# The residual's product on VectorE, four PSUM banks for the down-projection, and the second pair's weight-sum remainders on GpSimd, in a two-layer hybrid encoder step

## What is computed

```python
x = layer_norm(ALPHA * x + (1.0 + gate) * mix, ln_g, ln_b)
hin = x * (1.0 + scale) + shift
u = hin @ ffn_w_in + ffn_b_in              # 1024 -> 2 x 2816
u, hist = causal_dwconv(u, ffn_conv, ffn_conv_w)   # 3 taps
u = u + ffn_conv_b
f = (silu(u[..., :2816]) * u[..., 2816:]) @ ffn_w_down
x = layer_norm(ALPHA * x + (1.0 + gate) * f, ln_g2, ln_b2)
```

## Time and profile before

| | us |
|---|---|
| median of 3 runs (lowest to highest) | 3170.7 (3169.97 to 3174.64) |
| the profiled execution | 3175.71 |
| its span | 3173.9 |
| TensorE busy | 2951.9 (93%) |
| VectorE busy | 2312.7 (73%) |
| ScalarE busy | 1227.5 (39%) |
| GpSimd busy | 986.5 (31%) |
| one pass of the FFN loop (2806.54 to 2875.18) | 68.64 |

### The profile page before, as it was taken

How to read it: one execution, slowest core, us unless ns; L and a number is a source line. 1 busy time by engine, 2 the same in 40 slices (tenths; PEclk the granted TensorE clock), 3 DMA queues, 4 the chain that set the end, 5 groups by cost and what they waited for, 6 DMA issues and landing times. The chain is left out here.

```text
span 3173.9 us, 51760 instructions
## 1 busy us (share of the span) xinstructions
PE 2951.9 (93%) x18516; PEld 2792.6 (88%) x18516; DVE 2312.7 (73%) x3500; ACT 1227.5 (39%) x2360; POOL 986.5 (31%) x653
## 2 busy tenths in 40 slices
PE   7999989999998999999998879989998999999995
PEld 5999977999988999999997868878988999999994
DVE  7999966777459777788877556645277788887775
ACT  3333244554345332333333634444155333333224
POOL 2333435665315222223222121110323222222222
PEclk9999989999999999999999999999999999999998
DMA  6545653110111111111111210002201111111111
GB/s 265 176 171 180 227 193 109 54 54 21 54 34 34 47 53 40 45 48 46 46 46 35 90 42 34 35 28 79 78 21 47 41 47 46 48 44 52 41 40 56
DMA packets 86969, 225.75 MB, mean 71 GB/s; under 512 B 9388, under 2 KB 41076, under 8 KB 85812
## 3 DMA queue, kind: packets, MB, share of 16 engines
q1 hardware_dynamic: 46900, 139.10, 12.9%
q10 hardware_dynamic: 39936, 84.86, 7.8%
HBM read 192.59 MB, written 31.35 MB: 71 GB/s over the span
## 5 line engine op out<-in xcount | busy, mean ns | idle before, releaser
L370 POOL TENSOR_TENSOR WL<-RAW,WH 128x1024 fp32r<-128x1024 f32 x193 | 511.5, 2651 | 975.2 <-ACT WH L365 975.1
L374 PE MATMUL PS<-HH,WH 128*128 128x352 f32 x2120 | 704.1, 332 | 61.7 <-POOL WL L370 22.6
L378 PE MATMUL PS<-HH,WL 128*128 128x352 f32 x2120 | 689.8, 325 | 0.0
L377 PE MATMUL PS<-HL,WH 128*128 128x352 f32 x2120 | 689.3, 325 | 0.0
L374 PEld LDWEIGHTS PS<-HH,WH 128*128 128x128 f32 x2120 | 405.4, 191 | 79.4 <-issue 62.4
L2113 DVE SCALAR_TENSOR_TENSOR X<-PS,ADA,X 128x352 f32<-128x352 f32 (+1 forms) x704 | 326.7, 488 | 167.8 <-PE PS L378 162.5
L377 PEld LDWEIGHTS PS<-HL,WH 128*128 128x128 f32 x2120 | 406.4, 192 | 1.8
L378 PEld LDWEIGHTS PS<-HH,WL 128*128 128x128 f32 x2120 | 405.6, 191 | 0.0
L365 ACT ACTIVATE WH<-RAW 128x1024 fp32r<-128x1024 f32 x199 | 210.2, 1056 | 385.7 <-PE PS L374 378.8
L374 PE MATMUL PS<-FH,WH 128*128 128x352 f32 x960 | 325.2, 339 | 28.2 <-DVE X L2113 28.0
L378 PE MATMUL PS<-FH,WL 128*128 128x352 f32 x960 | 310.4, 323 | 0.0
(11 more groups left out here) (384 smaller groups left out, 6281.7 us busy)
## 6 DMA issues: line engine op xcount, KB each, us to landing
RAW<-ws SPq DMA_DIRECT2D x199, 512.0 KB, 3.3
ADR<-wada ACTq DMA_DIRECT2D x72, 512.0 KB, 4.8
scr<-V ACTq DMA_DIRECT2D x32, 528.0 KB, 3.0
X<-xT SPq DMA_DIRECT2D x3, 1408.0 KB, 20.7
OUTT<-scr SPq DMA_DIRECT2D x1, 4224.0 KB, 15.3
y<-X SPq DMA_DIRECT2D x3, 1408.0 KB, 5.5
AD0R<-wada SPq DMA_DIRECT2D x8, 512.0 KB, 13.3
AD<-wada SPq DMA_DIRECT2D x2, 2048.0 KB, 15.1
```

The costliest lines, as they stand in the source:

```text
L370: e.tensor_tensor(WL[u][:, :], RAW[:, u, :], WH[u][:, :].bitcast(fp32), ALU.subtract).then_inc(lo_done, 1)
L374: mm = e.matmul(out, WH[w][:, c:c + 128], mh, start=first, stop=False)
L377: e.matmul(out, WH[w][:, c:c + 128], ml, start=False, stop=False)
L378: return e.matmul(out, WL[w][:, c:c + 128], mh, start=False, stop=last)
```

## The change

Five edits. (1) `pool_normal` on GpSimd becomes `vec_normal` on VectorE, three instructions behind the first `t_lower`s and ahead of convolution (0,1); it waits for the reciprocal (`std_rdy`) instead of `hl_rdy`. (2) The down-projection of all pairs but the last uses the four banks 6, 7, 1, 5, and group k waits for update k-4; at k == 2 TensorE also waits until the next pair's second block has left banks 1 and 5. To make room, `up_first` writes groups into banks 0 to 5 in its own order, the mixed block (1,1) uses banks 1, 2, 3, 4, 0, and later blocks wait, before they reuse bank 1 or 5, for all 24 updates. (3) The remainders `S1L` to `S4L` of each second block (j,1) are made by GpSimd: three behind slab n+2, the fourth behind slab n+3; the first two wait also until the sum that reads the one they overwrite is made. (4) The sums and the remainders of the next first block stand behind updates 9, 11, ... 23 of `mix`. (5) In `first_half`, L2141 stands ahead of the gate, and the four sums follow the gate together.

```diff
@@ -622,11 +622,11 @@
                 for m in range(KB - 2 if q % 2 == 0 else 1, KB - 1):
                     pool_sum(p, q, m, ch)
 
-        def pool_normal(p, q, ch):
+        def vec_normal(v, q, ch):
 
             c0, cw = CHS[ch]
-            p.wait_ge(hl_rdy, low_count(HS[q], 2))
-            p.tensor_tensor(X[:, :, c0:c0 + cw], X[:, :, c0:c0 + cw], LN_R[q][ch][:, 0:cw].unsqueeze(1).to_broadcast([128, KB, cw]),
+            v.wait_ge(std_rdy, 6 * q + 2 * ch + 2)
+            v.tensor_tensor(X[:, :, c0:c0 + cw], X[:, :, c0:c0 + cw], LN_R[q][ch][:, 0:cw].unsqueeze(1).to_broadcast([128, KB, cw]),
                             ALU.mult).then_inc(nrl_rdy, 1)
 
         def vec_center(v, q, ch, b):
@@ -1681,6 +1681,7 @@
             if not isinstance(count, int) or count > 0:
                 need(e, s_, count)
 
+        DN_BANKS = (6, 7, 1, 5)
         FIRST_ORDER = [(0, 1), (1, 1), (0, 0), (0, 2), (1, 0), (1, 2)]
 
         def pe_ffn(e, l, n0, g0, hs):
@@ -1695,15 +1696,15 @@
             def up_first(n):
 
                 b = 3 * (g0 + up_index(1, 0, 0))
-                for half, ch in FIRST_ORDER:
+                for i, (half, ch) in enumerate(FIRST_ORDER):
                     if (half, ch) in ((0, 1), (1, 1)):
                         need(e, hi_done, n + half + 1)
                         need(e, lo_done, n + half + 1)
                     c0, cw = CHS[ch]
                     u = (n0 + half) % 2
-                    need(e, up_ev, b - 6 + 3 * half + ch + 1)
+                    need(e, up_ev, b - 6 + i + 1)
                     for k in range(KB):
-                        mm = three(e, PS[:, 3 * half + ch, 0:cw], u, k * 128, HH[:, k, c0:c0 + cw], HL[:, k, c0:c0 + cw],
+                        mm = three(e, PS[:, i, 0:cw], u, k * 128, HH[:, k, c0:c0 + cw], HL[:, k, c0:c0 + cw],
                                    k == 0, k == KB - 1, k == 0 and (half, ch) in ((0, 1), (1, 0)))
                     mm.then_inc(up_done, 1)
 
@@ -1734,7 +1735,7 @@
                 q, b = mixed_pair(l, j, f), 3 * (g0 + up_index(j, f, 0))
                 head = isinstance(j, int) and (j, f) == (1, 1)
                 ua, ub = n0 % 2, (n0 + 1) % 2
-                A, C, B, E0, E1 = (5, 2, 3, 4, 0) if f and not head else (0, 1, 2, 3, 4)
+                A, C, B, E0, E1 = (1, 2, 3, 4, 0) if head else (5, 2, 3, 4, 0) if f else (0, 1, 2, 3, 4)
                 T_ = [(XTH[i], XTL[i], 0, 0) for i in range(3)] + [(HH, HL, 0, CW)]
                 S_ = [(SH[i], SL[i], 0) for i in range(4)]
                 B11, B21, B22 = (HH, HL, 0, 0), (HH, HL, 4, 0), (HH, HL, 4, CW)
@@ -1751,10 +1752,14 @@
                 if not f:
                     need(e, up_ev, b)
                     need(e, st_dv, 3 * q)
-                free(3)
+                elif not head:
+                    need(e, dn_ev, d0 + 3 * KB * (j - 1))
+                free(2)
                 product(A, A11, B11, True, up_done, True)
 
-                free(1, (st_dv, 3 * q - 2))
+                free(3, (st_dv, 3 * q - 2))
+                if not f:
+                    need(e, dn_ev, d0 + 3 * KB * (j - 1))
                 need(e, sl_rdy, sl_count(l, q, 1))
                 if head:
                     need(e, sl_rdy, tl_count(l, 0))
@@ -1778,7 +1783,7 @@
 
                 need(e, hi_done, n + 2)
                 need(e, lo_done, n + 2)
-                free(2, (up_ev, b))
+                free(1, (up_ev, b))
                 whole(E1, ub)
 
                 need(e, up_ev, b + 4)
@@ -1802,9 +1807,11 @@
                     u = (n0 + m // 4) % 2
                     for ch, (c0, cw) in enumerate(CHS):
                         k = 3 * m + ch
-                        need(e, dn_ev, d0 + 3 * KB * j + k - 1)
+                        after(e, dn_ev, d0 + 3 * KB * j + k - 3)
+                        if k == 2:
+                            need(e, up_ev, 3 * (g0 + up_index(j + 1, 1, 0)) + 6)
                         for f in range(2):
-                            mm = three(e, PS[:, 6 + k % 2, 0:cw], u, f * 512 + (m % 4) * 128, FH[:, f, c0:c0 + cw],
+                            mm = three(e, PS[:, DN_BANKS[k % 4], 0:cw], u, f * 512 + (m % 4) * 128, FH[:, f, c0:c0 + cw],
                                        FLS[f][:, c0:c0 + cw], f == 0, f == 1, m % 4 == 0 and ch == 0 and f == 0)
                         mm.then_inc(dn_ps, 1)
 
...
@@ -1953,7 +1960,7 @@
                     for k in range(4):
                         sum_upper(1, 1, k)
                     upper(0, 1)
-                copy_out(1, 0, half, (ch,), b1 + i + 1)
+                copy_out(1, 0, half, (ch,), b1 + i + 1, i)
 
             def second_half(j, n, first=()):
                 split(n, 3)
@@ -2036,22 +2043,30 @@
             p.memset(UF[:, :, 0:GAP], 0.0)
             p.memset(UF[:, :, GAP + SEQ:GAP + UT - DEC - (FC - 1)], 0.0)
             params(0, 0)
-            pool_normal(p, 2 * l, 0)
             split(n0, 2)
             tails(0, 0)
-            pool_normal(p, 2 * l, 1)
             split(n0, 3)
-            pool_normal(p, 2 * l, 2)
             params(0, 1)
             split(n0, 4)
             tails(0, 1)
             split(n0, 5)
+            def sum_lower(j, f, i):
+
+                q = mixed_pair(l, j, f)
+                need(p, tap_sh_rdy, sh_count(l, q, i + 1))
+                if i < 2:
+                    need(p, ss_rdy, ss_count(l, q, 2 * i + 2))
+                p.tensor_tensor(SL[i][:, :], SF[i][:, :], SH[i][:, :].bitcast(fp32), ALU.subtract).then_inc(sl_rdy, 1)
+
             def pair(j):
                 n = n0 + 4 + 6 * (j - 1)
                 params(j, 0)
                 split(n, 2)
+                for i in range(3):
+                    sum_lower(j, 1, i)
                 tails(j, 0)
                 split(n, 3)
+                sum_lower(j, 1, 3)
                 params(j, 1)
                 split(n, 4)
                 tails(j, 1)
@@ -2105,21 +2120,21 @@
                 need(v, ft_rdy, x + 1)
                 v.tensor_tensor(FLS[f][:, :], FT[:, f, :], FH[:, f, :].bitcast(fp32), ALU.subtract).then_inc(fl_rdy, 1)
 
-            def update(j, k, m, ch):
+            def update(j, k, m, ch, banks=DN_BANKS):
 
                 c0, cw = CHS[ch]
                 need(v, dn_ps, d0 + 3 * KB * j + k + 1)
                 for a, w, st in pieces(c0, cw):
-                    ins = v.scalar_tensor_tensor(X[:, m, a:a + w], PS[:, 6 + k % 2, a - c0:a - c0 + w],
+                    ins = v.scalar_tensor_tensor(X[:, m, a:a + w], PS[:, banks[k % len(banks)], a - c0:a - c0 + w],
                                                  ADA[:, s, 2 * KB + m, st:st + 1], X[:, m, a:a + w], ALU.mult, ALU.add)
                 ins.then_inc(dn_ev, 1)
 
-            def mix(j, steps=iter(()), first=0):
+            def mix(j, steps=iter(()), places=range(1, 3 * KB, 3)):
 
                 need(v, x_rdy, 6 * l + 3)
                 for k in range(3 * KB):
                     update(j, k, k // 3, k % 3)
-                    if k % 3 == 1 and k >= first:
+                    if k in places:
                         next(steps, None)
                 for _ in steps:
                     pass
...
@@ -2178,6 +2193,13 @@
                 need(v, tap_sh_rdy, sh_count(l, mixed_pair(l, j, f), i + 1))
                 v.tensor_tensor(SL[i][:, :], SF[i][:, :], SH[i][:, :].bitcast(fp32), ALU.subtract).then_inc(sl_rdy, 1)
 
+            def w_splits(j):
+
+                yield from w_sums(j, 0)
+                for i in range(4):
+                    sum_lower(j, 0, i)
+                    yield
+
             def t_sums():
 
                 lq, mode = 2 * l, MODE[HS[2 * l]]
@@ -2254,21 +2276,19 @@
             gate(0, 0)
             for i in (0, 2, 1):
                 t_lower(i)
+            for ch in range(NCH):
+                vec_normal(v, 2 * l, ch)
             every_step(conv(0, 1))
             t_lower(3)
             v.wait_ge(nrl_rdy, 3 * l + 3)
             every_step(w_sums(1, 1))
             lower(0, 0)
             gate(0, 1)
-            for i in range(4):
-                sum_lower(1, 1, i)
             lower(0, 1)
 
             def second_half(j):
                 every_step(conv(j, 0))
                 mixed_out(j, 1, 0)
-                if not isinstance(j, int) or j > 1:
-                    sum_lower(j, 1, 3)
                 gate(j, 0)
                 mixed_out(j, 1, 1)
                 mixed_out(j, 1, 2)
@@ -2277,31 +2297,22 @@
                 every_step(conv(j - 1, 1))
                 mixed_out(j, 0, 0)
                 lower(j - 1, 0)
+                mixed_out(j, 0, 1)
                 gate(j - 1, 1)
-                steps = w_sums(j, 1)
-                next(steps)
-                next(steps)
-                mixed_out(j, 0, 1)
-                every_step(steps)
-                for i in range(3):
-                    sum_lower(j, 1, i)
+                every_step(w_sums(j, 1))
                 lower(j - 1, 1)
                 mixed_out(j, 0, 2)
             second_half(1)
```

(14 more changed lines are left out.)

## The result

The changed kernel takes 3092.35 us (median of 4 runs, 3091.86 to 3093.86) against 3170.99 (4 runs): a ratio of 0.9751, interval 0.9734 to 0.9768, 78.6 us less. The forecast was 3105.7 in a range of 3080 to 3135.

The account below looks back on a forecast made before the run. TensorE, busy 93% of the span, was taken as the bound. Loop passes 42, heads 13 and the down-projections beside pair 10 another 10 us made 65 us, forecasting 3105.7 us after allowing for the profiled execution's offset; range 3080 to 3135.

Parts of the forecast that it names:

- the heads: Start of each FFN: residual's product moved to VectorE shortens TensorE's 9.21 us gap and slow clock; 13 us for both.
- the down-projection beside pair 10: Down-projection with the convolution in it instead of sums: 4 to 6.5 us less, 5 taken; 10 us for both layers.
- the passes: FFN loop, 9 pairs in each of two layers: 2.35 us less per pass, 42 us in all.
- the wait ahead of A22: Second half of the up-projections: convolution ends later, so this product starts 0 to 0.9 us late; 0.4 taken per pass.
- 0.2 kept for latencies: FFN loop: part of the 2.95 us lost per pass that was not counted as gain.
- the time of one matmul: FFN loop: 0.161 us each, so 408 take 65.7 us and a pass of 68.64 loses 2.95.
- Four banks: Down-projection: waiting for update k-4 lets VectorE lag almost 3 us; with the sums spread, 2.1 us less per pass.
- the 0.83: Last product of a first pair: TensorE's wait goes when the evacuation stands ahead of the gate.
- The collision: Second pairs: GpSimd operations in flight hold up VectorE's two-SBUF-input operations and the reverse; convolution ends at 33.7 to 35.2 us.
- the 3.2 taken: FFN head: TensorE's new wait for the sixth slab's remainder on GpSimd, 0.5 to 3.2 us, upper end used.
- "Slower" by GpSimd's queue: Rival in the loop: five mean waits from 1.8 us make GpSimd's queue the bound; at 2.8 each, 3199; chance 0.04.
- Rival 1: Whole kernel: no new waits, GpSimd gets in between VectorE's operations, sixth slab misses the product; 3087; chance 0.25.

## Why the prediction was right, and where it was off

**Bound and stages.** TensorE bounds the kernel, and the measured time lies in the range. By the table the heads gave 15.1 us for 13 forecast, the down-projection beside pair 10 gave 10.7 for 10, and the passes 55.2 for 42. The error of 13 us is the passes': 2.35 us each forecast, 3.1 measured. The pass of 65.50 us also lies outside the 66.0 to 66.6 that the prediction gave as its sign.

**The failed terms of the pass.** Three sizes. "I take **0.4**" for the wait ahead of A22: it is 0. The convolution did end late, at 33.8 us from the start of the pass's first product, at the low end of the 33.7 to 35.2 worked out; and ScalarE's work behind it took 3.2 us (2716.26 to 2719.46) where the prediction counted 3.7. "0.2 kept for latencies": none was needed. The third is the time of one matmul: 0.161 us, rounded, made 65.7 us for a pass without waits, and the pass is at 65.50, which is 0.1605 for each of 408. Together 0.8 us in 18 passes, 14 us.

**Four banks.** Mechanism and size held: 2.13 us a pass with two banks instead. S3F met the slab's remainder as forecast (1.92 us), and four banks covered it. They also cover S1F at its old place: the move that the prediction gave a part in this is worth nothing by itself.

**L2141.** The prediction gave the 0.83 to the order alone. That step was too narrow: either the order or the earlier end of VectorE's list removes the wait, and only with both undone does it return, at 0.89. The sum was right because both edits were in the change.

**The remainders on GpSimd.** 1.34 us each was right: 1.31 where nothing is in the way. The collision was seen rightly, and charged to the wrong engine: it costs VectorE some 5 us a pass and TensorE nothing, where the prediction took 0.4. SBUF — State Buffer in the Trainium skill, section "Who interferes with whom", calls the shared ports an exclusive lock; FL at 2.35 and the four L2100 at 8.19 agree. GPSIMD Engine Reference in the Trainium skill, section "Engine selection", would keep the operation on VectorE; per instruction it is right (1.31 against 0.60), and the two placements take the same time.

**The head.** The size came out, its make-up only in part. As forecast, the sixth slab's remainder came behind the third product, with a slow stretch behind it. But the gaps, 4.27 and 3.40 us, are over the 3.2 taken, and the first is over the 0 to 3.5 given as a sign. The prediction had the slab's remainder itself ask during the third product; in fact the tails ahead of it in GpSimd's queue asked during the second, and stood until the third was done. The run with the third product later showed it, and took 7 us back. The 2 us gained ahead of slab n0+2 were not in the forecast at all; 1.8 of them came in the one head whose clock was granted in full.

**Rivals.** "Slower" by GpSimd's queue: its waits were 0.4 to 1.6 us each, not 1.8 or more, and the first remainder was ready 1.9 us before product C (2703.59 against 2705.50). Rival 1 at 3087 lay nearer than the forecast, in part by luck: its 49.5 us for the passes were too few (55.2) and its 22 for the heads too many (15.1). It was right that no new wait appears in the loop.

## What to carry to other kernels

Price each wait of the bounding engine by its own row, and then ask which edits remove it: two edits may each be enough, and then neither shows alone. A second pair of accumulation banks bought more here than any reordering, since it covered the 1.9 us that VectorE lost to a slab's remainder, wherever in the list that fell. Where two engines hold each other up, as VectorE and GpSimd do here, look before a long operation is placed at who stands in the other's queue behind it, and put it where nobody does.

## What the runs showed of the hardware

- VectorE's busy time holds waits for GpSimd. 6.2 us of operations with one SBUF input, put among those with two, moved the end of the convolution by 0.89 us.
- A GpSimd operation that asks while VectorE is at work may be passed by VectorE's next one: the tails asked at 987.31 in the second of three products and went behind the third, 4.35 us in all.
- Behind an idle time of 4.27 us TensorE's granted clock was 0.56 for the next 3.9 us; behind 3.40 us (second FFN) it was 0.66 for 4.0 us; behind one of 1.14 us it stayed at 1.00.
- The two heads of one execution were granted different clocks for the same 48 matmuls, behind nearly the same idle time: 1.00 behind 2.93 us (8.57 us for the stretch), 0.83 behind 2.82 us (10.05 us). Why is open.
